# Handing x over transposed in the first block of a one-core transformer-trunk kernel, with sums of squares by engines and a one-column product

## What is computed

```python
def rmsnorm(x, w):
    xf = x.astype(jnp.float32)
    y = xf * lax.rsqrt(jnp.mean(xf * xf, axis=-1, keepdims=True) + EPS)
    return (y * w.astype(jnp.float32)).astype(x.dtype)
...
        hn = rmsnorm(x, norm_w[l])
        proj = jnp.einsum('bsd,de->bse', hn, w_in[l])
        q, k, v, g_attn, h, c_gate, b_gate, g_conv = jnp.split(proj, SPLIT_POINTS, axis=-1)
        attn = swa_sink_attention(q, k, v, sinks[l], rel_bias)
        conv = short_gated_conv(h, c_gate, b_gate, conv_w[l], conv_b[l])
        mixed = jnp.concatenate([attn * jax.nn.silu(g_attn),
                                 conv * jax.nn.silu(g_conv)], axis=-1)
        x = x + jnp.einsum('bse,ed->bsd', mixed, w_out[l])
    return rmsnorm(x, final_norm_w)
```

## Time and profile before

| | |
|---|---|
| median of 3 runs | 1352.02 us (1351.94 to 1352.94) |
| the profiled execution's span | 1348.7 us |
| PE busy | 1331.5 us, 99% |
| DVE busy | 921.0 us, 68% |
| ACT busy | 537.9 us, 40% |
| POOL busy | 91.0 us, 7% |
| first product / first product of block 1 | 7.88 / 181.64 us |

### The profile page before, as it was taken

One profiled execution on the slowest core, in us unless ns is written; L12 is line 12 of the kernel. 1 busy time (PEld: TensorE's weight loads), 2 busy tenths in 40 slices (PEclk: granted clock), 3 DMA queues, 4 the chain that ended last, 5 costly groups with the idle time before them and its releaser, 6 DMA issues.

```text
span 1348.7 us, 16598 instructions
## 1 busy us (share of the span) xinstructions
PE 1331.5 (99%) x6034; PEld 1099.8 (82%) x6034; DVE 921.0 (68%) x1143; ACT 537.9 (40%) x939; POOL 91.0 (7%) x154
## 2 busy tenths in 40 slices
PE   9999999999999999999999999999999999999997
PEld 7778888888888888888888888878888888888886
DVE  6898976324477458984589855998439886656376
ACT  6754532322232433434334343343423444321454
POOL 0222312000000000000000000000000221200001
PEclk9999999999999999999999999999999999999999
DMA  9778995988978999869998799887898888899778
GB/s 330 301 284 286 404 378 181 296 311 298 331 251 254 294 277 293 252 216 312 297 291 249 222 289 295 283 257 238 296 323 310 318 269 279 288 316 359 276 254 307
DMA packets 206368, 390.02 MB, mean 289 GB/s; under 512 B 78848, under 2 KB 129104, under 8 KB 184656
## 3 DMA queue, kind: packets, MB, share of 16 engines
q1 hardware_dynamic: 186768, 321.83, 72.9%
q0 software_dynamic: 18304, 62.92, 12.8%
q10 hardware_dynamic: 1216, 4.21, 0.8%
HBM read 294.18 MB, written 98.93 MB: 291 GB/s over the span
## 4 chain that ended last, share of the span: by engine, by line
PE 88%; DVE 6%; issue 3%; DMA 2%; ACT 1%; SPq 0%; POOL 0%; DVEq 0%; ACTq 0%; POOLq 0%
PE banks L1933 85%; PE banks L1956 1%; PE banks L1968 1%; DVE w_ring L1312 1%; DMA qkv_park<-e 1%; PE banks L1977 1%; DVE raw L1386 1%; PE banks L1978 1%; DVE x_main L1320 0%; DVE raw L1392 0%; DVE e L1475 0%; PE banks L1857 0%; DMA x_far<-x_park 0%; DVE z L1359 0%; DMA raw<-in_w_in_dram 0%
## 5 line engine op out<-in xcount | busy, mean ns | idle before, releaser
L1933 PE MATMUL banks<-x_main,w_ring 128*128 128x512 f32 x2352 | 552.2, 392 | 3.2 <-DVE x_main L1320 2.8
L1933 PEld LDWEIGHTS banks<-x_main,w_ring 128*128 128x128 f32 x2352 | 437.8, 188 | 94.3 <-issue 4.8
L963 ACT ACTIVATE w_ring<-raw 128x1024 fp32r<-128x1024 f32 x224 | 236.5, 1056 | 554.9 <-PE banks L1933 540.6
L1312 DVE TENSOR_TENSOR w_ring<-raw,w_ring 128x1024 fp32r<-128x1024 f32 x224 | 274.2, 1224 | 212.1 <-ACT w_ring L963 211.8
L1933 PE MATMUL banks<-x_far,w_ring 128*128 128x512 f32 x1680 | 393.5, 391 | 0.7 <-DMA x_far<-x_park 0.6
L1933 PEld LDWEIGHTS banks<-x_far,w_ring 128*128 128x128 f32 x1680 | 313.0, 188 | 65.5 <-issue 0.8
L1933 PE MATMUL banks<-w_ring,x_main 128*128 128x512 f32 x1008 | 230.6, 389 | 0.8 <-DVE x_main L1320 0.8
L1933 PEld LDWEIGHTS banks<-w_ring,x_main 128*128 128x128 f32 x1008 | 189.1, 188 | 40.6 <-issue 1.2
L494 POOL DMA_DIRECT2D x_park<-x_main x104 | 56.0, 538 | 1014.1 <-DVE x_main L1320 1014.1
L989 ACT ACTIVATE x_main<-z 128x512 fp32r<-128x512 f32 x112 | 69.9, 625 | 130.0 <-issue 101.8
L1320 DVE TENSOR_TENSOR x_main<-z,x_main 128x512 fp32r<-128x512 f32 x112 | 76.9, 689 | 44.2 <-ACT x_main L989 44.1
(11 more groups left out here) (148 smaller groups left out, 852.9 us busy)
## 6 DMA issues: line engine op xcount, KB each, us to landing
x_far<-x_park SPq DMA_DIRECT2D x84, 1024.0 KB, 7.2
x_main<-x_park SPq DMA_DIRECT2D x84, 1024.0 KB, 7.4
x_park<-x_main POOLq DMA_DIRECT2D x104, 512.0 KB, 5.6
raw<-in_w_in_dram SPq DMA_DIRECT2D x128, 256.0 KB, 5.7
raw<-in_w_in_dram SPq DMA_DIRECT2D x32, 512.0 KB, 10.7
raw<-in_w_out_dram SPq DMA_DIRECT2D x32, 512.0 KB, 5.9
q_cur<-qkv_park SPq DMA_DIRECT2D x64, 128.0 KB, 5.6
z<-mix_park SPq DMA_DIRECT2D x16, 512.0 KB, 8.1
```

Source lines behind the costliest of these rows:

```text
L963: act.activation(w_ring[:, n % NW, :, 0, :], raw[:, c, k:k + 2, :], ACT.Copy).then_inc(w_hi_ready, 1)
L1312: dve.tensor_tensor(w_ring[:, n % NW, :, 1, :], raw[:, c, k:k + 2, :], w_ring[:, n % NW, :, 0, :], ALU.subtract).then_inc(w_lo_ready, 1)
L1933: op = pe.matmul(bank, left, right, start=(first and i == 0), stop=(kt == HK - 1 and i == 2), skip_group_check=goes_on)
```

## The change

The host hands over x a second time, transposed (`x_t`), and the parameters by columns (`col_params`). Block 0 loads `x_t` straight into `z`, so no transposes of x are left on PE. The feature factor is applied wherever x is split or taken (`x_hi`, `x_lo`, `place_0`, `t1_from_x`, `b21`, `t2`). Squares are made on the transposed x: six pairs of rows of h = 0 and all eight of h = 1 by ACT, two pairs by POOL; POOL and DVE add the pairs up, DVE folds them to one 128 x 512 tile, and PE sums over the partitions by four products with a column of ones (`sum_squares`). There are now two turns of factors. For h = 1 POOL multiplies x in `z` by the row factors, a pair of rows at a time (`factor_x1`), and `t1`, `x_hi` and `x_lo` of product 3 wait for it. The first weights come in two halves from ACT's DMA queue.

```diff
-ORDER0 = [*range(HK, KT), *range(HK)]
-BANK0 = {8: 4, 9: 5, 10: 6, 11: 7, 12: 4, 13: 5, 14: 6, 15: 7, 0: 4, 1: 5, 2: 6, 3: 7, 4: 6, 5: 7, 6: 6, 7: 7}
...
-FACTORS_AT = (3, 1)
...
+WARM = 7
+SQUARE0_AT = {(0, 3): (0,), (1, 0): (1,), (1, 3): (6,), (2, 0): (2, 3), (2, 1): (7,)}
...
+POOL_ADD1_AT = {(4, 1): 5, (5, 0): 0, (5, 2): 2}
+VAR_AT = {(3, 2): 0, (6, 0): 1}
+FACTORS_AT = {(3, 3): 0, (6, 2): 1}
+FACTOR1_AT = {(6, 2): 4, (7, 0): 5, (7, 2): 6, (8, 1): 7, (8, 3): 0, (9, 2): 1, (10, 1): 2, (11, 0): 3}
...
+            sp.dma_start(z[:, 0, HK:HK + 1, :], x_t[0, :, HK:HK + 1, :]).then_inc(x_first_loaded, 16)
...
+            def square_0(i, j):
+                pool.wait_ge(z_loaded[j], 16)
+                if j == 4:
+                    pool.wait_ge(x_first_loaded, 16)
+                pair = z[:, 0, 2 * j:2 * j + 2, :]
+                pool.tensor_tensor(squares[SLOT0[j]], pair, pair, ALU.mult).then_inc(squared_by_pool, 1)
...
+                pool.tensor_tensor(squares[0], squares[0], squares[SLOT0[j]], ALU.add).then_inc(added_by_pool, 1)
...
+                pool.tensor_tensor(squares[2], squares[2], squares[SLOT1[j]], ALU.add).then_inc(added_by_pool, 1)
...
+            def factor_x1(j):
+                pool.wait_ge(factors_ready, 2)
+                pair = z[:, 1, 2 * j:2 * j + 2, :]
+                pool.tensor_tensor(pair, pair, factor_row[1].unsqueeze(1).to_broadcast([P, 2, N]), ALU.mult
+                                   ).then_inc(x1_factored, 1)
...
-                act.activation(x_halves(n)[i][:, 0, :], z[:, h, kt16, :], ACT.Copy).then_inc(x_hi_ready, 1)
...
+                act.activation(x_halves(n)[i][:, 0, :], z[:, h, kt16, :], ACT.Copy, scale=scale).then_inc(x_hi_ready, 1)
...
+                if b == GATES and p in (2, 3):
+                    dve.scalar_tensor_tensor(out=half[:, 1, :], in0=z[:, h, kt16, :], scalar=norm_col[:, kt16:kt16 + 1],
+                                             in1=half[:, 0, :], op0=ALU.mult, op1=ALU.subtract).then_inc(x_lo_ready, 1)
...
+            def fold_squares(h):
+                to = squares[4 if h else 5]
+                dve.wait_ge(added_by_pool, 7 if h else 4)
+                dve.wait_ge(added_by_dve, 6 if h else 2)
+                dve.tensor_tensor(to, to, squares[2 if h else 0], ALU.add).then_inc(added_by_dve, 1)
+                dve.wait_ge(added_by_dve, 7 if h else 3)
+                dve.tensor_tensor(to[:, 0, :], to[:, 0, :], to[:, 1, :], ALU.add).then_inc(square_sum_ready, 1)
...
-                for t in range(4):
-                    op = pe.transpose(banks[:, bank, t * P:(t + 1) * P], x_cols[k // HK][:, t, k % HK * P:(k % HK + 1) * P],
-                                      ident[:, :])
-                op.then_inc(x0_turned, 1)
...
+            def sum_squares(h):
+                pe.wait_ge(square_sum_ready, h + 1)
+                if h == 1:
+                    pe.wait_ge(copy_ready, copy_count(GATES, 2, 0))
+                for t in range(4):
+                    op = pe.matmul(banks[:, FACTOR_BANK[h], t:t + 1], square_sum[h][:, t * P:(t + 1) * P], ones_col,
+                                   start=True, stop=True)
+                op.then_inc(var_summed, 1)
```

More of the change, by code:

```diff
@@ L213 @@
[L213 to L220, removed]
@@ new lines, in w_lo_first, with add_square @@
+            def w_lo_first(i):
+                dve.wait_ge(w_hi_ready if i else w_first_hi, 1)
+                dve.tensor_tensor(w_ring[:, 0, i, 1, :], raw[:, 0, HK + i, :], w_ring[:, 0, i, 0, :], ALU.subtract
+                                  ).then_inc(w_lo_ready if i else w_first_lo, 1)
+            def add_square(h, j):
+                to = squares[4 if h else 5]
+                i = (7, 1, 3).index(j) if h else (3, 7).index(j)
+                dve.wait_ge(squared_by_act, SQUARED[h, j])
+                if i > 0:
+                    dve.wait_ge(added_by_dve, (3 if h else 0) + i)
+                dve.tensor_tensor(to, to, squares[(SLOT1 if h else SLOT0)[j]], ALU.add).then_inc(added_by_dve, 1)
@@ L1415, in t2 @@
                 dve.wait_ge(t1_ready, t1_count(b, q))
-                dve.tensor_tensor(z[:, 1, high, :], z[:, 1, high, :], z[:, 1, k, :], ALU.subtract).then_inc(t2_ready, 1)
+                if b == GATES:
+                    for i in range(2):
+                        h = HK + 2 * q + i
+                        op = dve.scalar_tensor_tensor(out=z[:, 1, h, :], in0=z[:, 1, h, :], scalar=norm_col[:, h:h + 1],
+                                                      in1=z[:, 1, 2 * q + i, :], op0=ALU.mult, op1=ALU.subtract)
+                    op.then_inc(t2_ready, 1)
+                else:
+                    dve.tensor_tensor(z[:, 1, high, :], z[:, 1, high, :], z[:, 1, k, :], ALU.subtract).then_inc(t2_ready, 1)
             def t3(b, q):
@@ L1696, in _ @@
                         w_lo(W_LO_AT[n, quarter])
-                    if (n, quarter) == SQUARED_BY_DVE:
-                        square_last_low()
+                    for j in ADD0_AT.get((n, quarter), ()):
+                        add_square(0, j)
+                    if (n, quarter) == FOLD0_AT:
+                        fold_squares(0)
+                    for j in ADD1_AT.get((n, quarter), ()):
+                        add_square(1, j)
+                    if (n, quarter) == FOLD1_AT:
+                        fold_squares(1)
+                    if (n, quarter) in VAR_AT:
+                        x_variance(VAR_AT[n, quarter])
                     if quarter == 0:
@@ L1751, in _ @@
                             t1(b, l - 5)
-                        late = 1 if b == GATES else 0
+                        late = 2 if b == GATES else 0
                         if 7 + late <= l < 7 + late + QP:
```

439 lines of the change are left out of this document (181 added, 258 removed).

## The result

The changed kernel takes 1389.52 us (median of 4 runs, 1388.31 to 1392.98) against 1352.48 us (4 runs, 1351.94 to 1355.25) for the kernel before on the same chip: ratio 1.0274, 95% interval 1.026 to 1.0287. It is 37.0 us slower. 1380.0 had been forecast, with a range of 1361 to 1392.

What follows compares the result with a forecast made beforehand. DVE was taken to set the pace up to step 17: 5.0 start + 104.1 list + 5.0 chains + 37.4 POOL - 2.1 = 149.4 us, block 1 28.1 us later, span 1376.8, plus 3.3 gives 1380 us; range 1361 to 1392.

Steps and rivals of the forecast that it cites:

- DVE's list to step 17: Block 0, up to the second difference of step 17: DVE's queued instructions sum to 104.1 us, against 99.8 before.
- DVE idle (start 5.0, chains 5.0): Before step 17: DVE waits 5 us for first weights, 3 and 2 us for the two chains from squares to factors.
- POOL, net: Before step 17: 37.4 us of DVE delay from 17 POOL instructions, less 2.1 hidden by DVE instructions that read a bank.
- step 17 ready: Block 0: DVE ready for step 17 at 149.4 us; PE begins it at about 149.9, block 1 at 209.7.
- in the changed kernel these waits are short: DVE before step 17: of 20.3 us waited before, only 5 us at the start and two chains of 3 and 2 remain.
- The POOL term: Before step 12: each of 17 wide POOL instructions costs the full DVE queue 2.2 us by taking turns, 37.4 us altogether.
- The correction for instructions that read a bank: DVE's stretch before step 17: 14 instructions (8.4 us) run freely beside POOL, a quarter hidden, so 2.1 us subtracted.
- The clock: PE's waits in block 0: a granted clock under full pace would be one more loss that the sum lacks; no size given.
- The waits at the column products: Step 6 of block 0: PE waits some 10 us until DVE has folded the squares.
- the two-tensor means: Between 5 and 110 us: DVE instructions of two SBUF tensors average well above 1.22 and 0.69 us.
- POOL costs nothing: Rival, chance 0.05: POOL costs DVE nothing before step 17, which is ready at 117; 1347.5 us.
- stores late: Rival, chance 0.08: x stores behind POOL's multiplications hold the five x_main places, four steps about 3 us more each; 1392 us.

Runs made afterwards that it cites:

- tiny version: Changed kernel with its 17 POOL instructions of 128x1024 cut to 128x4 each, same places and waits, results wrong: 1364.32 us, ratio 1.0083.
- the memsets: Changed kernel with each of the 17 wide POOL instructions replaced by two memsets of the same tile, which read no SBUF: 1363.86 us, ratio 1.0081.
- the 17 on DVE: Changed kernel with POOL's 17 wide squares, additions and multiplications given to DVE: 1379.57 us, ratio 1.0202.
- the run without chains and with the load ahead: Changed kernel, 17 POOL instructions cut to 128x4, both factor rows turned from a constant column, one x_far load before the attention's first loads: 1356.14 us, ratio 1.0024.
- the kernel before with the load ahead: Kernel before, with only one x_far load put ahead of the attention's first loads in SP's queue: 1350.51 us, ratio 0.9983.

## Why the prediction was right, and where its terms were off

The sign, the mechanism and the place held; the sum was 10.8 us short at step 17, where DVE becomes ready, and 1.2 more behind it (61.5 us to block 1 where it had 60.3), which makes the 12.0 us by which block 1 came later than forecast.

| term | forecast | measured |
|---|---|---|
| DVE's list to step 17 | 104.1 | 106.3 |
| DVE idle (start 5.0, chains 5.0) | 10.0 | 26.6 (tiny version) |
| POOL, net | 35.3 | 27.3 |
| step 17 ready | 149.4 | 160.2 |

**Part of the agreement is luck.** The waits were 16.6 us too small and POOL's price 8.0 too large, and the two errors offset. With POOL's term right and the rest as it stood, the forecast would have been 1372 us; with the waits alone right, about 1397, above the range. The measured time lies half a microsecond inside the forecast's own 1368 to 1390.

**The step that failed** is "in the changed kernel these waits are short". By the prediction's own working DVE waited 20.3 us before, laid to x, turns and factors (by the trace it is 18.0, 120.1 less 102.10 busy), and all of it was let go. The start is nearly right (5.9 for 5.0), the chains cost 7.1 us in DVE's time (132.88 - 125.76) for 5.0, of which the second is the larger part. What was not counted at all are the waits for ACT: by the rows of the tiny version 1.4 us for the second piece of the first weights (7.4 - 6.0), 3.3 + 2.6 for high parts of x, 1.6 for squares and 1.3 for weights, 10.2 of the 16.6 us that are missing. The trace of before has waits for ACT too. DVE's waits up to step 17 there:

```profile
DVE x_main L1320 <- ACT x_main L989: 6.6, 8, 2.7
DVE z L1328 <- PE banks L1857: 4.9, 3, 2.8
DVE cols L1658 <- PE banks L2005: 3.0, 1, 3.0
DVE w_ring L1312 <- ACT w_ring L963: 1.9, 5, 0.9
DVE scratch L1687 <- PE banks L1873: 0.9, 1, 0.9
```

8.5 of these us end with ACT. They are not simply the same waits as in the changed kernel. Two of them (0.70 us each, at 17.26 and 20.80) follow an ACT instruction that had itself waited for turned x, and the longest (2.65 at 46.86) stands behind ACT's squares and its scaling of the second half, and this scaling is gone. The longest of this kind in the tiny version (2.61 at 43.84) follows an ACT instruction that had itself waited 2.97 us for PE. So the change took some waits for ACT away and brought others; no run separates them one by one. The wrong step was to put them at nothing, with 8.5 us of them in the trace.

**The POOL term** was the right mechanism, over-sized. 2.2 us a meeting is what the trace shows (3.36 - 1.22 = 2.1), but three meetings were no sample: over 17 instructions DVE loses 1.9 us each (32.5 / 17), and 0.3 of these fall into DVE's waits. The correction for instructions that read a bank (2.1) was right in kind. That POOL read and not merely worked or was late is shown by the memsets; that it is a bad trade even at DVE's own price, by the 17 on DVE.

**The clock** was named as a loss that the sum lacks. It is there (0.74 to 0.91 in every stretch from 20 to 140 us), and worth some 3 us, seen in the time only once the load is early.

**The rest.** Block 1 to the end passed the lateness on one to one, 40.1 us of it against 37.0 in the medians and 39.5 in the spans. The waits at the column products (9.24 us for "some 10") and the two-tensor means were as forecast; PE's waits did not come as 2 to 4 us at each of steps 9 to 16, but before steps 8, 10, 11 and 12 (5.61, 4.96, 4.52, 3.10) and then small (0.77, 0.23, 2.14). PE's first product came at 6.55, not at about 5. DVE's work behind step 17 is 52.6 us in both kernels, not 43; PE waits for none of it. "POOL costs nothing" is out by the tiny version: even there the change is 12.2 us slower, where the prediction had 1347.5, with some 13 us of waits for that case where its own sum has 10.0. So the change loses without POOL's price as well. What is left in the run without chains and with the load ahead is 5.6 us over the kernel before with the load ahead (1356.14 for 1350.51). At step 17 it is 5.7 us: 3.8 of a longer list (105.93 against 102.10 us busy) and 1.8 of more waiting. For "stores late" nothing speaks: no wait up to step 17 is put down to a store of x, and 7.7 us of waits of ACT without a releaser fall where DVE had work.

## What to carry to other kernels

An idle GpSimd is no free place for elementwise work beside a full VectorE: what it reads from SBUF takes VectorE's time. Here an instruction on GpSimd cost the kernel 1.5 us (25.2 / 17), and the same one on VectorE itself 0.9 (15.3 / 17). Before a change that takes work from TensorE, make the list of the engine that sets the pace and sum its waits by what releases them; when the cause of some of them goes away, ask what the engine will wait for in the new order. And when a gain at one place does not reach the end, look along the timeline for a wait that has grown: one load moved up in a queue let two such gains be seen in the time, and it made the kernel before 2.1 us faster, where the whole change made it slower.

## What was unexpected on the chip

Memsets of 128x1024 on GpSimd (0.95 us each, 34 of them) left VectorE's means at 1220 and 747 ns. TensorE's waits had unequal after-effects. A wait of 1.88 and one of 2.10 us for the same load, after a long stretch at full granted clock, were followed by 24 products in 7.3 us in place of 5.7. One of 1.90 us at that place in another run was followed by 24 in 5.73, and the 2.51 us of the earlier trace rows by 48 in 11.16. So the length of the wait alone does not tell; what decides it, no run here shows. Where it happens the price is clear: 1.7 us more, some seven products at the lower of the two levels of the clock, 1.2 GHz, by 0.23 us more for each.
